# A two-layer hybrid decoder step on one core: the side work of the projection stage is put on other slots and engines

## The reference, cut to what matters

```python
def decoder_layer(x, shift, wkv, sc_buf, ssm_conv, ssm, lp):
    x = x + 0.5 * swiglu(rmsnorm(x, norm_ffn1), ffn1_w_in, ffn1_w_out)
    h = rmsnorm(x, norm_mix)
    proj = h @ w_in                         # 1024 -> 6440 columns
    p_rwkv, p_sc, p_ssm = split(proj)
    y_rwkv, shift, wkv = rwkv7_mix(p_rwkv, shift, wkv, ...)
    y_sc, sc_buf = short_conv_mix(p_sc, sc_buf, ...)
    y_ssm, ssm_conv, ssm = mamba2_mix(p_ssm, ssm_conv, ssm, ...)
    x = x + concatenate([y_rwkv, y_sc, y_ssm]) @ w_out
    x = x + 0.5 * swiglu(rmsnorm(x, norm_ffn2), ffn2_w_in, ffn2_w_out)
```

## Time and profile before

| | |
|---|---|
| time, median of 3 runs | 1796.96 us (1795.07 to 1799.95) |
| profiled execution | 1796.79 us, span 1795.0 us |
| TensorE busy | 1609.0 us, 90% of the span |
| VectorE | 1002.9 us, 56% |
| ScalarE | 847.3 us, 47% |
| GpSimd | 634.2 us, 35% |
| mean granted TensorE clock | 0.954 |

### The profile page before, as it was taken

How to read it: one execution, slowest core, us unless ns; L and a number is a source line. 1 busy time by engine, 2 the same in 40 slices (tenths; PEclk the granted TensorE clock), 3 DMA queues, 4 the chain that set the end, 5 groups by cost and what they waited for, 6 DMA issues and landing times. The chain is left out here.

```text
span 1795.0 us, 41440 instructions
## 1 busy us (share of the span) xinstructions
PE 1609.0 (90%) x17389; PEld 1521.1 (85%) x17389; DVE 1002.9 (56%) x1700; ACT 847.3 (47%) x1472; POOL 634.2 (35%) x421
## 2 busy tenths in 40 slices
PE   5999988987779899999879999899786998899996
PEld 4999978985568788999879999888665887899995
DVE  4433377774669776443343434958554986654333
ACT  3444444665434454444344444546652445554431
POOL 1434422321056534344333443232212554334430
PEclk9999999998889999999989999999897999999998
DMA  5545564452044535555364554634501445455650
GB/s 167 188 148 193 161 178 142 131 176 64 3 112 128 169 103 167 187 174 187 102 202 142 188 191 142 188 119 146 171 1 33 140 124 155 133 181 175 203 171 24
DMA packets 280490, 256.28 MB, mean 143 GB/s; under 512 B 48022, under 2 KB 268540, under 8 KB 280290
## 3 DMA queue, kind: packets, MB, share of 16 engines
q1 hardware_dynamic: 276538, 252.05, 45.1%
q10 hardware_dynamic: 3768, 1.59, 0.3%
HBM read 242.22 MB, written 11.38 MB: 141 GB/s over the span
## 5 line engine op out<-in xcount | busy, mean ns | idle before, releaser
L210 POOL TENSOR_TENSOR front_lo<-front_raw,front_hi 128x1024 fp32r<-128x1024 f32 (+2 forms) x118 | 276.3, 2341 | 610.5 <-ACT front_hi L203 610.5
L223 PE MATMUL ps<-front_h_hi,front_hi 128*128 128x264 f32 x1520 | 454.9, 299 | 41.0 <-DVE front_lo L210 28.7
L224 PE MATMUL ps<-front_h_lo,front_hi 128*128 128x264 f32 x1520 | 442.8, 291 | 0.0
L225 PE MATMUL ps<-front_h_hi,front_lo 128*128 128x264 f32 x1520 | 442.6, 291 | 0.0
L203 ACT ACTIVATE front_hi<-front_raw 128x1024 fp32r<-128x1024 f32 (+2 forms) x238 | 246.5, 1037 | 298.6 <-PE ps L225 260.3
L223 PEld LDWEIGHTS ps<-front_h_hi,front_hi 128*128 128x128 f32 x1520 | 298.6, 196 | 50.4 <-issue 39.9
L210 POOL TENSOR_TENSOR out_lo<-out_raw,out_hi 128x1024 fp32r<-128x1024 f32 (+1 forms) x84 | 198.9, 2370 | 311.8 <-ACT out_hi L203 311.8
L224 PEld LDWEIGHTS ps<-front_h_lo,front_hi 128*128 128x128 f32 x1520 | 298.4, 196 | 1.2
L225 PEld LDWEIGHTS ps<-front_h_hi,front_lo 128*128 128x128 f32 x1520 | 296.6, 195 | 0.1
L203 ACT ACTIVATE out_hi<-out_raw 128x1024 fp32r<-128x1024 f32 (+1 forms) x168 | 173.2, 1038 | 219.9 <-PE ps L225 175.8
L210 DVE TENSOR_TENSOR front_lo<-front_raw,front_hi 128x1024 fp32r<-128x1024 f32 (+1 forms) x120 | 145.3, 1212 | 162.1 <-ACT front_hi L203 162.1
(11 more groups left out here) (366 smaller groups left out, 3399.2 us busy)
## 6 DMA issues: line engine op xcount, KB each, us to landing
front_raw<-in_w_in SPq DMA_DIRECT2D x50, 1024.0 KB, 5.2
front_raw<-in_ffn_w_in SPq DMA_DIRECT2D x44, 1024.0 KB, 5.9
out_raw<-in_ffn_w_in SPq DMA_DIRECT2D x44, 1024.0 KB, 5.5
back_sample_rows<-row_scratch SPq DMA_DIRECT2D x160, 128.0 KB, 3.0
out_raw<-in_w_out SPq DMA_DIRECT2D x16, 1024.0 KB, 5.2
front_raw<-in_ffn_w_out SPq DMA_DIRECT2D x16, 896.0 KB, 4.6
out_raw<-in_ffn_w_out SPq DMA_DIRECT2D x16, 896.0 KB, 4.6
front_raw<-in_ffn_w_out SPq DMA_DIRECT2D x8, 1024.0 KB, 5.0
```

The lines of the kernel that those rows point to most:

```text
L210: eng.tensor_tensor(self.lo[n % self.RING][:, 0:k, 0:w], self._raw(n), self.hi[n % self.RING][:, 0:k, 0:w].bitcast(F32), ALU.subtract).the ...
L223: pe.matmul(out, hi[:, j, 0:w], x_hi[:, j], start=start and j == 0, stop=False)
L224: pe.matmul(out, hi[:, j, 0:w], x_lo[:, j], start=False, stop=False)
L225: mm = pe.matmul(out, lo[:, j, 0:w], x_hi[:, j], start=False, stop=stop and j == k - 1)
```

## The change

- **Low parts.** The even projection tiles 4 to 12 and 48, 50 go from GpSimd to VectorE. VectorE makes its low parts three tiles ahead instead of four, and after the token shift instead of ahead of it; the one that lay among the last FFN tiles is left out there.
- **FFN tail.** The product of shift state and mu moves from the front of the projection into the FFN (`Vectors.dve`). The mean of the norm stands one tile later.
- **Convolution.** Tap 0 of each `xbc` tile goes to ScalarE (`tap0`), taps 1 to 3 stay on VectorE, one slot later. The scan's slots follow by one or two.
- **Samples.** `sample(m)` and `sample_out(m)` stand in one slot, 28 + 2m, ScalarE's part at 27 + 2m. Tanh and sigmoids of the low-rank inputs move to slots 21 and 23.
- **Roots.** The mean squares are read out of PSUM by VectorE (`sc_root`, `root`). One pass on ScalarE, three Ln and then three Exp, makes all roots ahead of `gates(4)`; both scalings on VectorE go to slots 48 and 50. Low-rank product p stands at slot 39 + p, gates at 40 + p, cumulation at 41 + p. The state stores 2 and 3 on SP go behind the low-rank loads.
- **Block boundary.** All shift rows go into the back stage's groups 0 and 1: transposes, copies (a ring of four) and 14 stores. The decays and weighings of pair 0 and the copies of the sample vectors are done at the end of the front stage in buffers of their own; the sample vectors are transposed ahead of the first gram.

```diff
+            if mt % 2 == 0 and mt < KT - 2:
                 ws.split_lo(dve, n + 5)
...
-            if n == 1:
+            if n == self.mean_after:
                 norm.pe_mean(pe)
...
+        mu = env.col("rwkv_mu", 0, XT).unsqueeze(2).to_broadcast([P, XT, NS])
+        dve.tensor_tensor(env.shift[:], env.shift[:], mu, ALU.mult).then_inc(self.derived, 1)
...
+def conv_prompt(dve, s, dst, src, taps, width, done, first=0):
...
+    for j in range(first, width):
...
-        ws = Stream(st, KT, pieces, halves, raw_ring=3, on_dve={0, *range(1, len(halves), 2)})
+        ws = Stream(st, KT, pieces, halves, raw_ring=3, on_dve={0, *range(1, len(halves), 2),
+                                                                    *range(base + 4, base + 14, 2), *range(base + 48, base + H, 2)})
...
+                    yield 35
+                    for m in range(2, 4):
+                        sp.wait_ge(s("hst_done"), m + 1)
+                        sp.dma_start(hs_out[m], hst[:, m]).then_inc(s("state_out"), 16)
...
+                    yield 50
+                    pool.wait_ge(s("hfin_stored"), 16)
+                    pool.wait_ge(s("first_pq"), 2)
+                    pool.wait_ge(s("nb_done"), 1)
+                    c4 = lambda a: a.rearrange("p (c t) -> p c t", c=NCH)
+                    dec, inv = mix.pq0[:, 0], mix.pq0[:, 1, :, 1:C + 1]
+                    for out, x0, x1 in ((mix.bk0[:, 0], mix.nb[:, 0, 0:T], inv), (mix.bk0[:, 1], k[:, 0, 0:T], inv),
+                                        (mix.ar0[:, 0], mix.kkn[:, 0, 0:T], dec[:, :, 0:C]),
+                                        (mix.ar0[:, 1], r[:, 0, 0:T], dec[:, :, 1:C + 1])):
+                        pool.tensor_tensor(c4(out), c4(x0), x1, ALU.mult).then_inc(s("first_weighed"), 1)
+                    pool.wait_ge(s("nb_done"), 2)
+                    pool.wait_ge(s("k_done"), RT)
+                    for i, x0 in ((0, mix.kkn), (2, mix.nb), (3, k), (4, r)):
+                        pool.tensor_copy(mix.vecs[:, :, i], x0[:, :, T:N]).then_inc(s("vecs"), 1)
 
                 more = Part(side(pool))
                 for n in range(H):
...
+                    for slot in range(2, 12):
+                        yield slot
+                        if slot < 10:
+                            i = slot - 2
+                            act.wait_ge(evicted, i + 2)
+                            act.activation(xa[:, i, 0:T], xbc[:, i, 0:T], ACT.Copy, scale=env.col("ssm_conv_w", i)).then_inc(s("tap0"), 1)
+                        if slot >= 4:
+                            i = slot - 4
+                            act.wait_ge(s("xconv"), 3 * (i + 1))
+                            act.activation(xa[:, i, 0:T], xa[:, i, 0:T], ACT.Silu,
+                                           bias=env.col("ssm_conv_b", i)).then_inc(s("xa_done"), 1)
...
+                    act.wait_ge(samples, 1)
+                    act.activation(mix.xs[0:64, 24], mix.xs[0:64, 24], ACT.Tanh).then_inc(s("lr_done"), 1)
...
+                        if p == 4:
                             act.wait_ge(s("norm_max"), RT)
+                            act.wait_ge(s("ssm_read"), 2)
                             act.wait_ge(s("ln_bias"), 1)
                             act.activation(nrm[:], nrm[:], ACT.Ln, scale=LN_SCALE).then_inc(s("norm_ln"), 1)
-                            act.wait_ge(s("norm_ln"), 1)
+                            act.activation(sc_root[:], sc_root[:], ACT.Ln).then_inc(s("norm_ln"), 1)
+                            act.activation(root[:], root[:], ACT.Ln).then_inc(s("norm_ln"), 1)
...
+                            act.activation(sc_root[:], sc_root[:], ACT.Exp, scale=-0.5).then_inc(s("norm_inv"), 1)
+                            act.activation(root[:], root[:], ACT.Exp, scale=-0.5).then_inc(s("norm_inv"), 1)
+                        gates(p)
+                    yield 48
+                    act.wait_ge(s("cum_sum"), RT)
+                    act.wait_ge(s("lora_ps"), 3 * RT)
+                    for i, sign in enumerate((-DECAY, DECAY)):
+                        act.activation(mix.pq0[:, i], mix.cum[:, 0], ACT.Exp, scale=sign).then_inc(s("first_pq"), 1)
+                    act.activation(mix.vecs[:, :, 1], mix.sws[:], ACT.Exp, scale=-DECAY).then_inc(s("vecs"), 1)
...
-                        yield i + 1
+                        yield i + 2
                         dve.wait_ge(evicted, i + 2)
+                        dve.wait_ge(s("tap0"), i + 1)
                         done = conv_prompt(dve, s("xconv"), xa[:, i, 0:T], xbc[:, i], lambda j: env.col("ssm_conv_w", 8 * j + i),
...
-                        yield 27 + 2 * m + m // 2
+                        yield 28 + 2 * m
                         sample(m)
-                        yield 28 + 2 * m + m // 2
                         sample_out(m)
+                        yield 29 + 2 * m
...
+                    dve.tensor_scalar(sc_root[:], ps[:, EB, 0:N], D / SC, NORM_EPS, ALU.mult, ALU.add).then_inc(s("sc_read"), 1)
...
+                        if slot == 43:
+                            weigh_bonus(0)
+                            weigh_bonus(1)
+                        if 44 <= slot < 50:
+                            weigh_bonus(slot - 42)
+                        if slot == 46:
+                            normed_keys(0)
+                            minus_b(0)
+                        if slot == 47:
+                            normed_keys(1)
+                        if slot == 48:
+                            dve.wait_ge(s("norm_inv"), 3)
...
-                    if n % 2 == 1:
-                        ws.split_lo(dve, base + n + 4)
...
+                    if n + 3 < H and ws.on_dve[base + n + 3]:
+                        ws.split_lo(dve, base + n + 3)
...
+                    for slot in range(39, 51):
+                        yield slot
+                        if slot < 47:
+                            p, c = slot - 39, slice((slot - 39) * P, (slot - 38) * P)
...
-                    pool.wait_ge(s("pq_done"), 2 * p + 2)
+                    pool.wait_ge(s("pq_done"), 2 * p)
...
+                    if g == 0:
+                        shift_rows(0)
+                        shift_rows(1)
+                        shift_rows(2)
...
+                    if g < 2:
+                        shift_store(3 * g)
+                        if g == 1:
+                            shift_rows(4)
...
+                for m in range(RT):
+                    mm = pe.transpose(ps[0:V * NS, UB + m // 4, m % 4 * P:m % 4 * P + P],
+                                      vecs[:, m].rearrange("p v b -> p (v b)"), ident)
+                mm.then_inc(s("vecs_ps"), 1)
```

More of the change, by code:

```diff
@@ L632, in _ @@
                     dve.tensor_copy(ys[:, k * P:(k + 1) * P], ps[0:NS, b + 2, 0:P]).then_inc(copied, 1)
-def conv_prompt(dve, s, dst, src, taps, width, done):
-    for j in range(width):
+def conv_prompt(dve, s, dst, src, taps, width, done, first=0):
+    for j in range(first, width):
         x = src[:, j:j + T]
@@ L642, in conv_prompt @@
         else:
-            dve.wait_ge(s, done + j)
+            if j > first:
+                dve.wait_ge(s, done)
             dve.scalar_tensor_tensor(out=dst, in0=x, scalar=taps(j), in1=dst, op0=ALU.mult, op1=ALU.add).then_inc(s, 1)
-    return done + width
+        done += 1
+    return done
 def conv_sample(dve, s, dst, tmp, srcs, taps):
@@ L760, in side @@
                     yield 31
-                    for m in range(4):
-                        if m == 2:
-                            yield 37
+                    for m in range(2):
                         sp.wait_ge(s("hst_done"), m + 1)
@@ L914, in side @@
                     act.dma_start(d["s_conv"][layer].rearrange("b j f -> (b j) f"), cv_rows[3:27, :]).then_inc(s("rows_stored"), 16)
-                    yield 39
-                    act.wait_ge(s("sc_scaled"), ST)
-                    for g in range(2):
-                        act.wait_ge(s("ssm_ms"), g + 1)
-                        act.activation(root[:, g], ps[:, B + g, 0:N], ACT.Ln, bias=env.eps[:, 0:1], scale=D / 256).then_inc(s("ssm_ln"), 1)
-                    act.wait_ge(s("ssm_ln"), 2)
@@ new lines, in side @@
+                        if slot == 43:
[10 more added lines that the diff above has]
+                            dve.wait_ge(s("norm_inv"), 3)
+                            for i in range(ST):
+                                dve.scalar_tensor_tensor(out=acc[:, i], in0=acc[:, i], scalar=env.col("sc_norm", i), in1=sc_root[:],
+                                                         op0=ALU.mult, op1=ALU.mult).then_inc(s("sc_scaled"), 1)
@@ L1203, in _ @@
+                        if slot == 49:
+                            minus_b(1)
+                        if slot == 50:
+                            for m in range(4):
+                                dve.scalar_tensor_tensor(out=ym[:, m], in0=ym[:, m], scalar=env.col("ssm_norm", m), in1=root[:, m // 2],
```

(36 more changed lines are left out.)

359 lines of the change are left out of this document (161 added, 198 removed).

## The result

The changed kernel takes 1755.68 us (median of 4 runs, 1752.43 to 1757.02) against 1796.78 (1795.07 to 1799.95): a ratio of 0.9767, 95% interval 0.9747 to 0.9786. The forecast was 1757. The profiled execution has a span of 1750.6 us at a granted clock of 0.966 (before: 1795.0 and 0.954). The total is right; the parts are not all, and part of their errors cancel.

The account below looks back on a forecast made before the run. TensorE, busy nine tenths of the span, was taken as the bound. Gains of 1.4 + 9.4 + 5.7 + 3.4 + 0 = 19.9 us per layer, twice 40, took the 1795.0 span to 1755, hence 1757 us; range 1733 to 1783.

Parts of the forecast that it names:

- part 2: Projection tiles 3 to 16: long taps go, tile 16 starts 47.5 us behind tile 3 instead of 58.2; 9.4 us a layer gained.
- part 6: First pairs behind the gram: waits and transposes go, shift-row copies, issues and transposes come; 0 net, 3 gained to 4 lost.
- Part 1: Tail of the FFN: low part and shift-state product leave VectorE's chain, so projection tile 3 starts 1.4 us earlier.
- Part 3: Tiles 26 to 43: root passes and low-rank pause go, sample chain adds pauses; 93.8 us instead of 99.6, 5.7 gained.
- caught once: Samples, tiles 26 to 43: a GpSimd low part slows one addition before sum 0, which ends at 22.7 us.
- Rival (a): Less is gained, 1774 to 1790 us: two more sample catches (4.6), first pairs 4, weighings 2.7 per layer; chance 0.18.
- Part 4: Tiles 44 to 50: the pass of roots makes TensorE wait 5.2 us instead of 2.6; block ends at 52.9 us.
- rival (e): Roots on ScalarE: one table load serves Ln and Exp, as the skill says; 1754 us, chance 0.02.
- Part 5: Block boundary: gram 56 us after tile 43's end instead of 59.5; 3.4 us a layer gained together with part 4.
- I put 4.5 of it on the path: First pairs: of the added shift-row copies, issues and transposes, 4.5 us were to lengthen the path.
- (c): Only trades waits: VectorE leads tiles 3 to 16 as before since ScalarE's tap 0 comes late; 1799 us, chance 0.04.
- (d): Slower: GpSimd catches VectorE's added low parts in slots 14 to 46, 2.0 us each; 1817 us, chance 0.05.

## Why the prediction was right, and where it was not

**What bounded the kernel.** Right: TensorE's work is the same, and the gain came out of its pauses and of work at the lower clock. That the total came within 1.3 us of the forecast is in part luck: part 2 gave 3.2 and 1.5 us a layer more than its sum and part 6 some 3 more, parts 1 and 3 together some 3 less, and the end of the kernel took back 3 in all in this profile.

**Part 1** failed in one step. "The mean after tile 2 changes nothing: it stays ahead of what needs it" was taken for the projection's norm; it is the FFN's. Its root then starts 3.6 us later; ScalarE stands for it, the high and low parts behind it come later, and TensorE stands 1.16 us at 46.97. With the slow matmuls around it, tile 3 of the FFN takes 4.5 us instead of 2.9, and the whole FFN is 2.1 and 2.9 us longer. What the sum did count gave more than its 1.4: from the projection's first tile to tile 3 it takes 12.6 us in both layers, where it took 15.0 and 16.0. It would have been more still, had GpSimd not caught the low part of h: the two L259 take 3.07 us in the first row here, and 0.89 before. The second row is the sample addition of part 3.

```profile
230.73 3.07 DVE L259 SCALAR_TENSOR_TENSOR front_h_lo<-x,cols,front_h_hi 128x264 fp32r<-128x264 f32 x2
...
342.82 3.42 DVE L1022 TENSOR_TENSOR sample_state<-sample_state,outer 128x1024 f32<-128x1024 f32 x1
```

**Part 2** had the mechanism right (the runs with the low parts on GpSimd and with tap 0 on VectorE give 3.8 and 2.4 to 4.0 us a layer back) and the size too small: 12.6 and 10.9 with the moved piece, for 9.4. The mis-sized terms are the pauses left, put at 1.5 and measured at 0.6, the 1.3 us for half clock, and VectorE's lead: at 3.05 us a slot it was to hold TensorE for eight slots, but tiles 4 to 6 follow each other at 2.90. Windows of all engines (PE, PEld, DVE, ACT, POOL) over tiles 3 to 16, after and then before; behind them TensorE alone over the first 42 us from the gram (busy with count, granted clock, DMA share, GB/s):

```profile
245.00:290.00 45.00, 44.28 (x348) 42.50 (x348) 42.28 (x78) 29.80 (x47) 7.41 (x3) 1.00 0.71 211
...
478.00:520.00 42.00, 36.81 (x967) 0.98 0.53 141
```

```profile
245.00:303.00 58.00, 49.82 (x349) 46.87 (x351) 48.73 (x83) 27.57 (x41) 16.80 (x7) 0.91 0.56 164
...
498.00:540.00 42.00, 35.73 (x871) 0.87 0.47 127
```

The granted clock was 0.91 over that stretch before and is 1.00 after: once the pauses are gone, so is the half clock, all of it.

**Part 3** was forecast at 5.7 and gave 3.2 and 3.7. The first pause has the predicted size (4.5 for 4.6), the second is 0.9 us longer than its 4.5, and the low-rank inputs' 8.6 is gone. The step that failed is "caught once": all eight additions are caught, since each stands right behind VectorE's own low part, at the moment when GpSimd has begun the next tile's. In the kernel before six of eight took 1.22. The sum of sample 0 ended 22.7 us behind tile 25's end, as forecast with its one catch; that of sample 2 ended at 45.5 and not at 41.9, since samples 1 and 2 were caught too. With no addition caught the stretch takes 88.6 and 89.4 us, and the prediction's own sum for that case, 93.8 less 4.6, is 89.2. Rival (a) had this mechanism.

**Part 4.** Right in the numbers that can be compared: the pass of roots begins 1.7 us behind tile 43's end and holds the gates up as the sum said.

```profile
424.14 1.28 ACT L943 ACT_TABLE_LOAD   x1
...
428.27 1.28 ACT L947 ACT_TABLE_LOAD   x1
...
432.48 1.28 ACT L839 ACT_TABLE_LOAD   x1
...
433.78 0.47 ACT L839 ACTIVATE cum_decay<-ps,cols 128x256 f32<-128x256 f32 x1
```

The gates start at 433.78, 11.3 us behind tile 43's end at 422.46, and TensorE waits 5.5 us where 5.2 was forecast. Three table loads are there: the Exp behind the Ln has its own. So the rule of the Trainium skill (ScalarE: Activation LUTs, section Table sets: the hidden batching unit), that one set holds both, does not give this program the saved load, and rival (e) falls.

**Part 5** is right in sum (3.8 and 3.1 for 3.4). The gram starts 55.6 us behind tile 43 where 56 was forecast. But most of it is VectorE's: its overfull slots 45 to 51 beside a hole of 10 us in slot 44 cost 6 us a layer, which the sum counted (28 us of slots) without asking what else could hold them.

**Part 6** was wrong in size: 0 was forecast, and the two profiles give 6.1 and 3.3. The 6.1 rests on the low 119.9 us of one profile. The kernel before and the run that gives it the low parts alone take 125.5 and 127.5 us in the mean, the nine profiles with the changed back stage 122.5 and 124.1, so the gain is about 3 us a layer. "I put 4.5 of it on the path" is the step: the 4.8 us of the wait for sample rows and of the late transposes went, and the shift rows put some 2 in their place. In layer 0 the clock behind the gram is 0.98 instead of 0.87, after a boundary pause of 5.7 instead of 9.3 us, and 0.94 with the pause at 10.4. How much of the 3 us is the clock alone was not separated.

**The rivals.** (c) and (d) fell: collisions were fewer in tiles 3 to 16 and more in the samples. Some eight VectorE instructions a layer are caught in the stretch, four of them in the samples; (d) needed ten more than the sum counted.

## What to carry to other kernels

Before work is put on an engine, look at what runs on GpSimd at that moment: a VectorE instruction with two SBUF inputs that starts beside one lost 2.0 to 2.2 us here, more than the whole instruction, so it can pay to give the faster engine more work. When TensorE's wait names one engine, follow that engine's own wait before moving anything; a slot moved on TensorE alone only moved the pause. And look for the hole first: one of the two large gains behind the change (6 us a layer; the other is the low parts of tiles 32 to 38, with 7) came from placing existing VectorE work into an idle stretch next to the overfull one.

## What the runs showed of the hardware that was not expected

- A GpSimd subtraction of 128 x 1024 and VectorE's two-input instructions hold each other up in both directions: the eight caught additions took 3.38 to 3.43 us (1.22 with GpSimd idle), and GpSimd's own instruction beside them 2.75 to 3.04 us instead of 2.4. In the rows here GpSimd's begins inside VectorE's low part, and VectorE's addition of 342.82 begins inside GpSimd's. The addition ends at 346.24, 1.08 us behind GpSimd's end at 345.16, and in the other three of layer 0 this distance is 1.08 to 1.09 too: almost all of the addition's 1.22 us comes when GpSimd is through, so a catch costs about what is left of GpSimd's instruction.

```profile
341.69 1.22 DVE L210 TENSOR_TENSOR front_lo<-front_raw,front_hi 128x1024 fp32r<-128x1024 f32 x1
...
342.12 3.04 POOL L210 TENSOR_TENSOR front_lo<-front_raw,front_hi 128x1024 fp32r<-128x1024 f32 x1 [3.72 <-ACT front_hi L203]
```

- Less work for TensorE came with a lower clock: without the shift rows the granted clock behind the gram was 0.92 and 0.85 in the two layers instead of 0.98 and 0.97.
- The last pauses in a stretch are worth more than their length: tile 3 to 16 lost 7.5 us of pauses and 12.6 us of time (13.5 less the piece that moved on).
